# Gathering the first expert block inside the router, and stacking the halves of h in second blocks' down product

## The chip, the cores and the metric

One core of one Trainium2 chip runs the whole kernel, in one launch. The metric is the device time of that launch in microseconds; of several runs the median is given.

## The reference, cut to what matters

One inference step of a hybrid decoder layer over T = 1056 tokens (1024 of a prompt, 32 of samples). The change touches the last part, a mixture of 16 experts with top-2 routing, and the tables that lead to it:

```python
h = rmsnorm(x)
# top-1 group of 4, then top-2 of 4 experts in it; weights wts
# token-expert pairs sorted by expert into blocks of rows
out = (silu(xb @ w_eg[e]) * (xb @ w_eu[e])) @ w_ed[e]     # D=1024, FF=512
x = x + sum over the two pairs of a token (weight * out)
y = rmsnorm(x)                                            # final norm
```

All is fp32. Ahead of it stand an SSM and a gMLP mixer and a cross-attention, which the change leaves alone.

## The kernel before, in words

A product keeps fp32 accuracy on TensorE by splitting both factors into a high part (rounded to the fp32r format by a copy on ACT) and a low part (the rest, a subtraction on DVE), and summing three products: high x high, high x low and low x high (`product`, L4036 to L4038).

**The router's block** (`router_programs`, L3183) makes the normed rows h, stores them to DRAM (`h_scr`, SP, L3298) and computes the choice of experts. Its tail is a long chain of small operations on DVE: picks (L3605 to L3634), a prefix sum over tokens on PE (L3450, L3453), counts and block starts (L3645 to L3656), a slot for each token-expert pair (L3657 to L3663), its fields (L3665 to L3680), and one-hot matrices of block and lane (L3681 to L3687; POOL makes one third, L3357). Eighteen products on PE (L3462) turn these into tables: `m.tab` and `m.row`, the row that each lane of each block holds, and `m.tw`, its weight (DVE, L3689 to L3692). `keep_busy` (L129) issues idle products on PE. SP loads the six 1 MB pieces of expert 0's weights (four of gate and up, two of down) while that goes on (`load_piece`, L3756). Then all engines meet at a barrier.

**The experts' block** (`stage_experts`, L3763). Each expert has one block of 128 lanes and, if it has more rows, blocks of 64 lanes ahead of it (called second blocks here; `m.more` says how many). A block goes through these steps:

- POOL reads the block's column of `tab` and gathers its rows of `h_scr` into `e_x` (`gather`, L3922, L3925); PE turns them (`turn`, L4023); ACT and DVE split them into `e_xT` (`turned`, L4157, L4294).
- PE multiplies by gate and up (`hidden`, 48 products of 512 columns). A second block has only 64 lanes, so the high and low halves of x stand side by side as 128 lanes (`hidden_split`, L4063, L4064, 32 products) and DVE adds the two halves of the result (`gated_split`, L4311 to L4321).
- SiLU on ACT, the product with up on DVE; PE turns h (`turn_h`, L4104); ACT and DVE split it (`e_hT_high`, `e_hT_low`, L4325; for second blocks at the even lanes alone, L4330).
- PE multiplies by down (`down`, 24 products for a block of either kind). ACT scales the result by `m.tw` into `e_out` (`out`, L4202), POOL adds it by an indirect DMA to `res_scr` (`finish`, L3935) and waits until it has landed.

PE is one block ahead of itself: it takes the hidden product of block b+1, then the down product of block b, then turns h of b+1. The weights of the next expert are split meanwhile: a piece is loaded (SP), its high half made (ACT, L4157), its low half (DVE, L4298, for down pieces L4336), and the raw piece is then free, which lets SP load the same piece of the expert after. For expert e, `down_parts` waits on ACT for the down product of the expert before. The order on each queue is the order of the code: on ACT in a second block SiLU, x high, `out`, the down pieces, h high; on DVE in an expert's last block two low halves, the gating, x low, two low halves, h low.

At the start of the experts' block nothing of expert 0 is split yet, and its first rows are not gathered: POOL issues gathers 0 to 2 behind one another; PE runs 23 idle products (46 matmul instructions in the trace), turns block 0, runs 6 more, and starts. The second block's lanes are placed at even lane numbers, which the tables take into account:

```python
            g.keep_busy(UP, 23)
            turn(0)
            g.keep_busy(UP, 6)
            hidden(0, 0)
```

At the end the last two blocks are added without a trip through `res_scr`, and the final norm follows.

## Time and profile before

| | us |
|---|---|
| median of 3 runs | 1991.69 |
| lowest and highest | 1988.87 and 1991.7 |
| the profiled execution, its own time | 1985.8 |
| its span in the profile | 1983.7 |
| PE busy in the span | 1911.1 |
| DVE, ACT, POOL busy | 1015.7, 753.6, 410.3 |
| mean granted clock of TensorE | 0.989 of full |
| router's block ends, experts' block starts | about 1551.1 |
| first product of the experts | 1561.44 |

All times inside the profile are us from the start of the span. A matmul's own duration overlaps the next one's, so the distance from start to start is what a product costs. "Idle before" names the engine whose work ended the wait, and "issue" a wait for nothing that the profile shows.

### The profile page before, as it was taken

How to read it: one execution, taken by the hardware profiler on the slowest of the kernel's cores; microseconds unless marked ns; L12 is line 12 of the kernel's file. 1: busy time of each engine (PE TensorE's matmuls, PEld its weight loads, DVE VectorE, ACT ScalarE, POOL GpSimd, SP SyncE). 2: the span in 40 equal slices, each digit the busy share in tenths (PEclk: the TensorE clock that was granted, in tenths of full speed). 3: DMA queues.
4: the chain of work that ended last, by engine and by line, in shares of the span. 5: the costliest groups of instructions: out<-in, count | busy, mean ns of one | idle time of the engine just before them, and what ended most of it. 6: DMA issues, size and time to landing. Idle time of an engine off the chain costs nothing. (4 is left out here: it accounts for less than half of the span.)

```text
span 1983.7 us, 32313 instructions
## 1 busy us (share of the span) xinstructions
PE 1911.1 (96%) x11976; PEld 1717.4 (87%) x11977; DVE 1015.7 (51%) x1221; ACT 753.6 (38%) x1105; POOL 410.3 (21%) x513
## 2 busy tenths in 40 slices
PE   7999999999999999999999999999999799999995
PEld 5888999999999999889998899888788788887884
DVE  4314355554556565556114431445544666785786
ACT  4322132222244444633112232433321455774674
POOL 2000100000245455551011000000100222242225
PEclk9999999999999999999999999999999899999998
DMA  6121233334244434498434120446125387998997
GB/s 205 63 92 65 75 85 87 94 85 113 81 130 121 142 113 136 127 339 279 148 105 153 54 78 28 159 171 255 35 96 222 118 287 236 367 391 295 314 318 277
DMA packets 224593, 324.33 MB, mean 163 GB/s; under 512 B 15149, under 2 KB 158029, under 8 KB 224449
## 3 DMA queue, kind: packets, MB, share of 16 engines
q1 hardware_dynamic: 189924, 271.96, 40.2%
q0 software_dynamic: 7344, 25.38, 4.9%
q10 hardware_dynamic: 27232, 25.66, 3.7%
q8 instruction: 69, 1.13, 0.2%
q14 instruction: 24, 0.20, 0.0%
HBM read 250.97 MB, written 73.28 MB: 163 GB/s over the span
## 5 line engine op out<-in xcount | busy, mean ns | idle before, releaser
L4157 ACT ACTIVATE e_w_high<-big 128x2048 fp32r<-128x2048 f32 x94 | 175.5, 1910 | 37.7 <-PEq L3704 20.7
L286 PE MATMUL psum<-hT_high,t_w_high 128*128 128x352 f32 x528 | 171.2, 324 | 0.0
L288 PE MATMUL psum<-hT_high,t_w_low 128*128 128x352 f32 x528 | 170.1, 322 | 0.0
L287 PE MATMUL psum<-hT_low,t_w_high 128*128 128x352 f32 x528 | 170.1, 322 | 0.0
L4298 DVE TENSOR_TENSOR e_w_low<-big,e_w_high 128x2048 fp32r<-128x2048 f32 x64 | 143.8, 2288 | 34.8 <-ACT e_w_high L4157 27.4
L286 PE MATMUL psum<-hT_high,scan_w_high 128*128 128x352 f32 x384 | 131.3, 342 | 0.0
L288 PE MATMUL psum<-hT_high,scan_w_low 128*128 128x352 f32 x384 | 124.5, 324 | 0.0
L287 PE MATMUL psum<-hT_low,scan_w_high 128*128 128x352 f32 x384 | 123.8, 322 | 0.0
L4036 PE MATMUL psum<-e_w_high,e_xT 128*128 128x512 f32 x272 | 107.4, 395 | 3.1 <-DVE e_xT L4294 3.0
L4038 PE MATMUL psum<-e_w_high,e_xT 128*128 128x512 f32 x272 | 106.2, 390 | 0.0
L4037 PE MATMUL psum<-e_w_low,e_xT 128*128 128x512 f32 x272 | 106.0, 390 | 0.0
L286 PE MATMUL psum<-r_w_high,hT_high 128*128 128x512 f32 x256 | 101.8, 398 | 4.3 <-DVE hT_low L720 4.3
L287 PE MATMUL psum<-r_w_low,hT_high 128*128 128x512 f32 x256 | 100.7, 393 | 0.0
L288 PE MATMUL psum<-r_w_high,hT_low 128*128 128x512 f32 x256 | 100.7, 393 | 0.0
L286 PEld LDWEIGHTS psum<-hT_high,t_w_high 128*128 128x128 f32 x528 | 99.1, 188 | 0.1
L287 PEld LDWEIGHTS psum<-hT_low,t_w_high 128*128 128x128 f32 x528 | 99.1, 188 | 0.0
L288 PEld LDWEIGHTS psum<-hT_high,t_w_low 128*128 128x128 f32 x528 | 99.1, 188 | 0.0
L4336 DVE TENSOR_TENSOR e_w_low<-big,e_w_high 128x2048 fp32r<-128x2048 f32 x30 | 67.9, 2290 | 46.2 <-ACT e_w_high L4157 46.2
L1082 DVE SCALAR_TENSOR_TENSOR t_conv_out<-t_conv_in,veca,t_conv_out 128x1080 f32<-128x1080 f32 x60 | 80.6, 1344 | 7.5 <-DVE t_conv_out L1080 1.2
L1525 DVE TENSOR_SCALAR s_att<-psum 128x768 f32<-128x768 f32 x32 | 30.6, 958 | 100.0 <-PE psum L1333 100.0
L286 PE MATMUL psum<-yT_high,m_w_high 128*128 128x352 f32 x252 | 81.6, 324 | 0.0
L287 PE MATMUL psum<-yT_low,m_w_high 128*128 128x352 f32 x252 | 81.4, 323 | 0.0
(623 smaller groups left out, 4970.9 us busy)
## 6 DMA issues: line engine op xcount, KB each, us to landing
big<-in_w_expert_gate SPq DMA_DIRECT2D x32, 1024.0 KB, 7.1
big<-in_w_expert_up SPq DMA_DIRECT2D x32, 1024.0 KB, 10.1
big<-in_w_expert_down SPq DMA_DIRECT2D x32, 1024.0 KB, 12.0
t_w<-in_w_in SPq DMA_DIRECT2D x24, 512.0 KB, 4.7
m_gates<-gate_scr SPq DMA_DIRECT2D x22, 528.0 KB, 4.6
x_scr<-t_conv_out ACTq DMA_DIRECT2D x20, 512.0 KB, 4.8
gate_scr<-s_gate_tanh ACTq DMA_DIRECT2D x16, 528.0 KB, 3.3
scan_w<-in_w_gate SPq DMA_DIRECT2D x16, 512.0 KB, 4.1
```

Source lines behind the costliest of these rows:

```text
L286: nc.tensor.matmul(out, ah, w_h, start=start, stop=False)
L287: nc.tensor.matmul(out, ah, w_l, start=False, stop=False)
L288: return nc.tensor.matmul(out, al, w_h, start=False, stop=stop)
L1082: op = nc.vector.scalar_tensor_tensor(o, c[:, j:j + CB_OUT], wk[j], o, ALU.mult, ALU.add)
L1525: nc.vector.tensor_scalar(att[:, q].rearrange("p (b r) t -> p b (r t)", b=2), ps[:, RB:RB + 2, 0:XW], 0.0, None, ALU.min).then_inc(s_mn, 1)
L4036: nc.tensor.matmul(ps[:, bank, :], ah[:, k, :], w_h, start=(k == 0), stop=False)
L4037: nc.tensor.matmul(ps[:, bank, :], ah[:, k, :], w_l, start=False, stop=False)
L4038: mm = nc.tensor.matmul(ps[:, bank, :], al[:, k, :], w_h, start=False, stop=(k == kt - 1))
L4157: return nc.scalar.activation(dst, src, ACT.Copy)
L4298: nc.vector.tensor_tensor(wl[:, p, :], raw[:, p, :], wh[:, p, :].bitcast(F32), ALU.subtract).then_inc(s_wl, 1)
L4336: nc.vector.tensor_tensor(wl[:, p, :], raw[:, p, :], wh[:, p, :].bitcast(F32), ALU.subtract).then_inc(s_dl, 1)
```

## The change

First half. The 128 lanes of block 0 hold the first tokens of expert 0, in order, so they can be known from the prefix sums alone, without the tables. In the router's block, DVE makes a one-hot of each pick's place in expert 0, PE sums it into a row index with nine two-column products, POOL gathers the rows, PE turns them, and ACT and DVE split them. ACT also makes the high halves of expert 0's four gate and up pieces there, and DVE the first low half. The tiles for that get fixed addresses (`FirstBlock`). POOL also turns the table of steps so that it accounts for the moved lanes. The idle products at the start of the experts' block go.

Second half. For second blocks of experts 1 to 14, h is split into `e_hT_high`'s lanes 0 to 63 (high) and 64 to 127 (low), so that the down product is 16 products (`down_split`), and DVE adds the two halves (`out_summed`) before ACT scales 64 rows (`out_split`). Since the results now stand at lanes 0 to 63 and no longer at the even ones, four small products and a chain on DVE (`lanes_moved`) make a table for the scatter (`tab_o`) and move `m.tw`, at the start of the experts' block.

```diff
 router, POOL
+            pool.wait_ge(s_inl, 1)
+            nc.gpsimd.tensor_scalar(more0[:], nbk[:, 0:1], float(BASE), None, ALU.mult).then_inc(s_pv, 1)
...
+            nc.gpsimd.tensor_scalar(back[:], step[:], more0[:, 0:1], -float(BASE), ALU.is_le, ALU.mult).then_inc(s_pv, 1)
...
+            pool.wait_ge(ahead.s_index, 3)
+            for q in range(2):
+                pool.wait_ge(s_xst[q], 16 * ((NT + 1 - q) // 2))
+            nc.gpsimd.indirect_dma_start(
+                out=ahead.x[:], out_offset=None, in_=g.h_scr,
+                in_offset=bass.IndirectOffsetOnAxis(ap=idx0[:, 0:1], axis=0)).then_inc(ahead.s_x, 16)
 router, PE
+            pe.wait_ge(ahead.s_index, 1)
+            for c in range(NT):
+                mm = nc.tensor.matmul(ps[:, CN, 0:2], ahead.lanes[:, c, :], row0[:, c, :], start=(c == 0), stop=(c == NT - 1))
+            mm.then_inc(ahead.s_index, 1)
             g.keep_busy(3, 32)
+            pe.wait_ge(ahead.s_x, 16)
+            for k in range(DK):
+                at_k = (k % 2 * (DK // 2) + k // 2) * P
+                tr = nc.tensor.transpose(ps[:, TQ + k // 4, (k % 4) * P:(k % 4 + 1) * P], ahead.x[:, at_k:at_k + P], g.ident[:])
+            tr.then_inc(ahead.s_xt, 1)
             pe.wait_ge(s_ohl, 1)
 router, ACT
+            for p in range(ahead.HIGHS):
+                act.wait_ge(g.s_piece[p], 16)
+                nc.scalar.activation(ahead.wh[:, p, :], g.pieces[:, p, :], ACT.Copy).then_inc(ahead.s_wh, 1)
+            act.wait_ge(ahead.s_xt, 1)
+            nc.scalar.activation(ahead.xhl[:, :, 0, :], first_turned, ACT.Copy).then_inc(ahead.s_xh, 1)
 router, DVE, behind the prefix sums
+            ch.done(nc.vector.scalar_tensor_tensor(lane0, before0, 1.0, both[:, 0:NT, 0], ALU.add, ALU.mult))
+            nc.vector.scalar_tensor_tensor(ahead.lanes[:], mid(lane[:], NT), 1.0, last(lane0, P),
+                                           ALU.add, ALU.is_equal).then_inc(ahead.s_index, 1)
...
+            dve.wait_ge(ahead.s_index, 2)
+            ts(idx0[:], ps[:, CN, 0:1], float(T), None, ALU.add).then_inc(ahead.s_index, 1)
...
+            dve.wait_ge(ahead.s_wh, 1)
+            tt(ahead.wl[:, 0, :], g.pieces[:, 0, :], ahead.wh[:, 0, :].bitcast(F32), ALU.subtract).then_inc(ahead.s_wl, 1)
             dve.wait_ge(s_tb, 1)
...
+            dve.wait_ge(ahead.s_xh, 1)
+            tt(ahead.xhl[:, :, 1, :], first_turned, ahead.xhl[:, :, 0, :].bitcast(F32), ALU.subtract).then_inc(ahead.s_xl, 1)
 experts, POOL
-            for b in range(3):
+            pool.sem_inc(s_ix, 1)
+            for b in range(1, 2):
                 gather(b)
...
+            gather(2)
+            pool.wait_ge(s_lx, 9)
...
+            pool.wait_ge(s_far, MOVED)
 experts, PE
+            def down_split(b):
+                pe.wait_ge(s_hl, b + 1)
+                pe.wait_ge(s_oc, b)
+                for j in range(2):
+                    for k in range(FK):
+                        q, at = GU + k // (FK // 2), (k % (FK // 2)) * D + j * BANK
+                        nc.tensor.matmul(ps[:, DN + j, :], hth[:, k, :], wh[:, q, at:at + BANK], start=(k == 0), stop=False)
+                        mm = nc.tensor.matmul(ps[:, DN + j, :], hth[:, k, :], wl[:, q, at:at + BANK], start=False,
+                                              stop=(k == FK - 1))
...
-            g.keep_busy(UP, 23)
-            turn(0)
-            g.keep_busy(UP, 6)
+            lanes_moved()
             hidden(0, 0)
...
                 with pe.If(n > 0):
-                    with pe.Fori(0, n) as i:
+                    hidden_split(e, behind + 1)
+                    down(behind)
+                    turn_h(behind + 1)
+                with pe.If(n > 1):
+                    with pe.Fori(1, n) as i:
                         b = within(behind + i)
                         hidden_split(e, b + 1)
-                        down(b)
+                        down_split(b)
                         turn_h(b + 1)
                 b = within(behind + n)
                 hidden(e, b + 1)
-                down(b)
+                with pe.If(n > 0):
+                    down_split(b)
+                with pe.If(n < 1):
+                    down(b)
 experts, ACT: in an expert's last block, behind h_high(b)
+                    with act.If(n > 0):
+                        out_split(b)
+            def out_split(n):
+                act.wait_ge(s_ds, n + 1)
+                nc.scalar.activation(ob[0:XR], ob[0:XR], ACT.Copy, scale=m.tw[0:XR, bass.ds(n, 1)]).then_inc(s_oc, 1)
 experts, DVE: in an expert's last block, behind h_low(b)
+            def out_summed(b):
+                dve.wait_ge(s_dn, b)
+                dve.wait_ge(s_of, b)
+                nc.vector.tensor_copy(ob[0:XR], flat(ps[XR:P, DN:DN + 2, :])).then_inc(s_da, 1)
+                dve.wait_ge(s_da, b + 1)
+                nc.vector.tensor_tensor(ob[0:XR], ob[0:XR], flat(ps[0:XR, DN:DN + 2, :]), ALU.add).then_inc(s_ds, 1)
 experts, DVE, start
+            low(0, 1)
+            low(0, 2)
             nc.vector.tensor_scalar(far[:], m.row[:], float(SEQ), FAR, ALU.is_lt, ALU.mult).then_inc(s_far, 1)
...
-            low(0, 0)
-            low(0, 1)
-            turned(0)
-            low(0, 2)
             low(0, 3)
+            lanes_moved()
```

`lanes_moved` on PE is four products with 48 columns; on DVE it is ten small operations and two over 768 elements, the last two behind POOL's one-column copies (`s_lx`).

## Rows read from the trace of the kernel before

**Rows 1.** Page, part 1: busy time, share of the span and instructions of each engine.

```profile
PE 1911.1 (96%) x11976; PEld 1717.4 (87%) x11977; DVE 1015.7 (51%) x1221; ACT 753.6 (38%) x1105; POOL 410.3 (21%) x513
```

**Rows 2.** Windows: each engine's busy time (instructions), then granted clock, DMA share, GB/s.

```profile
1672.00:1684.00 12.00, 12.00 (x60) 10.03 (x58) 8.73 (x5) 9.14 (x7) 4.90 (x4) 1.00 0.54 125
1692.00:1804.00 112.00, 110.03 (x519) 91.00 (x518) 86.31 (x53) 75.38 (x54) 35.97 (x25) 1.00 1.03 377
```

**Rows 3.** Waits of PE from 1560 to the end: us in total, times, longest.

```profile
PE psum L4036 <- DVE e_xT L4294: 3.0, 2, 1.9
PE psum L4036 <- DVE e_hT_low L4330: 1.9, 1, 1.9
PE psum L4063 <- issue: 1.2, 1, 1.2
```

**Rows 4.** Chain of waits in order of time, at the seam: start, length, what.

```profile
1551.27 6.93 PE psum L129 x46
1558.20 0.89 PE psum L4023 x8
...
1560.16 1.24 DVE e_xT L4294
...
1561.44 0.50 PE psum L4036
```

**Rows 5.** Timeline, end of the router's block and start of the experts', by engine.

```profile
1545.89 4.08 PE L3462 MATMUL psum<-o_block_onehot,o_lane_onehot 128*128 128x144 f32 x18 [5.79 <-DVE o_block_onehot L3686]
...
1541.00 1.37 DVE L3682 TENSOR_TENSOR o_lane_onehot<-o_lane_of,o_lanes 128x1152 fp32r<-128x1152 f32 x1
...
1550.02 0.27 DVE L3689 TENSOR_SCALAR tab<-psum,o_spare_row 128x48 uint32<-128x48 f32 x1 [3.00 <-PE psum L3462]
...
1551.17 3.71 ACT L4157 ACTIVATE e_w_high<-big 128x2048 fp32r<-128x2048 f32 x2 [20.75 <-PEq L3704]
...
1552.55 1.27 POOL L3925 DMA_INDIRECT e_x<-h_scr,e_idx  x1 [0.95 <-POOL e_idx L3922]
```

**Rows 6.** Windows of low granted clock (the third value from the right is the clock's).

```profile
1544.30:1554.50 10.20, 7.32 (x33) 7.18 (x34) 5.46 (x11) 3.33 (x2) 1.48 (x2) 0.50 0.00 0
1810.50:1813.90 3.40, 3.40 (x10) 2.62 (x9) 3.40 (x3) 3.40 (x4) 3.02 (x2) 0.50 0.35 93
```

**Rows 7.** Groups by form from 1551 to 1940: busy, mean ns, idle before.

```profile
L4157 ACT ACTIVATE e_w_high<-big 128x2048 fp32r<-128x2048 f32 x94 | 175.5, 1910 | 37.7 <-PEq L3704 20.7 <-DMA big<-in_w_expert_down 12.3 <-DMA big<-in_w_expert_gate 3.5
L4298 DVE TENSOR_TENSOR e_w_low<-big,e_w_high 128x2048 fp32r<-128x2048 f32 x64 | 143.8, 2288 | 34.8 <-ACT e_w_high L4157 27.4 <-issue 7.4
...
L4311 DVE COPY e_silu<-psum 64x512 f32<-64x512 f32 x6 | 4.2, 693 | 8.4 <-PE psum L4064 5.6 <-issue 2.8
```

**Rows 8.** Timeline around the second of the six second blocks, PE, DVE; SP at the third.

```profile
1651.00 0.27 PE L4023 MATMUL psum<-ident,e_x 128*128 128x128 f32 x1
...
1657.37 0.60 PE L4104 MATMUL psum<-ident,e_h 128*128 128x128 f32 x4
1657.73 0.48 PE L4063 MATMUL psum<-e_w_high,e_xT 128*128 128x512 f32 x1
...
1659.37 0.69 DVE L4325 TENSOR_TENSOR e_hT_low<-psum,e_hT_high 128x512 fp32r<-128x512 f32 x1
...
1682.66 0.38 SPq L3756 DMA_DIRECT2D big<-in_w_expert_gate  x1
```

**Rows 9.** Timeline, POOL's gather with least room and the transposes that use its rows.

```profile
1863.42 1.00 POOL L3925 DMA_INDIRECT e_x<-h_scr,e_idx  x1 [0.80 <-POOL e_idx L3922]
...
1873.91 1.03 PE L4023 MATMUL psum<-ident,e_x 128*128 128x128 f32 x8
```

**Rows 10.** DMA from 1624 to 1936: every queue with packets, MB, share; a gather's landing.

```profile
q1 hardware_dynamic: 21138, 81.51, 67.3%
q0 software_dynamic: 5219, 19.02, 24.2%
...
e_x<-h_scr,e_idx POOLq DMA_INDIRECT x18, 7.4
```

171 lines of the change are left out of this document (133 added, 38 removed).

## The prediction, made blind

> **What bounds the kernel now.** I read the page first: PE is busy for 1911.1 us of the span [rows 1], so almost nothing can be won but by giving PE less to do or by closing its few gaps. Both halves of the change lie in the last fifth: the first is about the seam between the router's block and the experts' block, the second about PE's products inside the expert loop. Next I read the experts' stretch by the share of the DMA engines. Just before 1684 us they are half idle (0.54, 125 GB/s), then they are full for 112 us at a stretch (1.03, 377 GB/s) [rows 2]. In that stretch the weights set the pace and PE runs beside them. The waits of PE say where it shows: 3.0 us on the split x (two waits, both around the first blocks), 1.9 us in one wait on the split h behind late down weights, 1.2 us of issue at one branch, and nothing else of size until the end [rows 3]. The seam is seen best in the chain of waits: from the start of the experts' block to the first product it is 6.93 us of idle products that only keep PE busy, 0.89 of transposes, ACT's and DVE's split of x (from 1559.09 to 1561.40), in all 10.17 us from 1551.27 to 1561.44 [rows 4]. PE waits there for a gather that POOL could issue only at 1552.55 [rows 5].
>
> **The first half, step by step.** Taken off the path: the gather, its transposes, the split of x and the wait for them, 10.17 us. Put on it:
> - DVE, before the tables: one comparison over 128x1152 as in L3682, 1.4 us, and two small operations of about 0.2 (L3689 takes 0.27 with 48 columns) [rows 5]: 1.8 us, and all behind it on DVE moves by that, with POOL's products and PE's table product.
> - The low half of x at the end of DVE's router program, 1.24 us [rows 4], behind the tables, and so ahead of the barrier.
> - Four small products (the lanes' move) on PE ahead of the first real one, each at about 0.11 us by the eight transposes in 0.89 [rows 4], some 0.5.
>
> So PE would restart at 1551.27 + 1.8 + 1.24 = 1554.3 and reach its first product at 1554.9 in place of 1561.44: 6.5 us earlier.
>
> Costed at nothing: the four high halves of the weights on ACT (4 x 1.91 [rows 7]) lie in ACT's 20.75 us of idleness [rows 5]; the first low half on DVE (2.29 [rows 7]) lies in the 3.00 us in which DVE waits for the table product [rows 5]. The three low halves left for the new block need 2.3, 4.6 and, behind three small operations, 7.5 us, and PE asks for them 2.8, 5.5 and 8.3 us after its first product (12 products of 0.23 each time [rows 8]), itself 0.6 after the start. That cover is thin: each is ready about a microsecond early or less. The gather moves to about 1539; by its old landing (issued 1552.55, used from 1558.20 [rows 4, 5], 5.6 us) its rows are there by 1545, when PE is idle anyway ahead of the table product (5.79 us [rows 5]). The table of moved lanes on DVE is two operations over 768 elements (about 0.9 each by L3682) and some ten of 0.2, nearly 4 us, so DVE is done about 11.5 us into the block; PE's first two products take 11 us, and the gate times up needs DVE only after them. POOL waits for it before its loop; its first scatter is due later still. Its eight one-column copies move from behind the second gather to ahead of the third, and must only finish before DVE's last two of these operations. SP's first weight loads of the next expert depend on DVE's low halves and go out about 1 us earlier to 5 us earlier, into DMA engines that have room.
>
> What must be paid back is the clock. TensorE's granted clock is 0.50 from 1544.3 to 1554.5, that is 1.2 GHz, since PE had nothing to do ahead of the table product; it was back at 2.4 GHz after PE had run its idle products for 3.3 us [rows 4, 6]. Those paid for the rise before; now the first real products will. A second low stretch, after the 1.9 us wait, lasted 3.4 us [rows 6]. At half speed such a stretch costs 1.7 us. I take it once. The Trainium skill, "TensorE: Matmul & The Clock Gate", section on what the clock gate does, says that the array falls to half rate when it has been idle and comes back only after it has been kept busy; by that rule, too, dropping the warm-up is not free, and without it the first half would be worth the full 6.5. Bounds: 0 (clock stays up, because the transposes now break the idle time) to 3.4 us (two stretches). First half: 6.5 - 1.7 = **4.8 us**.
>
> **The second half.** A down product of a second block is 16 products of 512 columns in place of 24. From the start of the transposes of x (1651.00) to that of the transposes of h (1657.37) are 6.37 us; less 0.89 for the eight transposes [rows 4], the 24 products take 5.5 us [rows 8], 0.23 each; eight less save 1.84. Six second blocks ran (DVE's 64-row copies come six times [rows 7]), each the only one of its expert: 11.0 us off PE. What comes back:
> - The third of them lies just ahead of the 112 us in which the DMA engines are full [rows 2]. The next weights are issued at 1682.66, just ahead of the transposes that end the hidden product [rows 8], so their place is set before this down product is begun; PE 1.84 us earlier behind it only waits 1.84 longer, where the 1.9 us wait is now [rows 3]. Lost: 1.8.
> - The fourth stands right behind that wait, with DVE running late on low halves: I take off 0.6.
> - The output of a second block: before, ACT alone, in one pass over 128x1024; now DVE copies and adds 64x1024 from PSUM, then ACT scales. 64x512 take 0.69 [rows 7], so each of the two is between 0.69 and 1.39; near the upper end, 1.25, since it is a length of data that doubles: 2.5 us, and on ACT 1.1 (over half of the 1.91 that 2048 columns take [rows 7]). It lies beside PE's next hidden product, 7.3 us of work or more, and the next down product needs it only then. But DVE does it behind its last low half of h, which at the second of the six ends at 1660.06 [rows 8]: 1660.06 + 2.5 + 1.1 = 1663.7, against 1657.37 - 1.84 = 1655.5, + 0.4 + 7.4 + 0.9 = 1664.2 (transposes, 32 products, transposes), when PE wants the banks. Half a microsecond to spare, three times (where experts with two blocks follow each other). Queued behind it: on ACT the next SiLU, which must wait for DVE anyhow; on POOL the scatter, about 2 us later, and with it a gather. That gather had 10.5 us to its transposes at the tightest place [rows 9], and among the experts it lands in 7.4 [rows 10]; 10.5 - 1.8 - 1.7 = 7.0. I take off 0.5 for both.
> - Two more branches in each of the 14 rounds. Lower end: 0 (L4104 to L4063, with a loop's end and branches between, takes 0.36, no more than four transposes [rows 8]); upper end: 1.23 each, the issue wait [rows 3]. Near the lower, 0.1, in ten rounds: 1.0. The Trainium skill, "Advanced Engine Details and Errata", Control Flow Timing, gives 108 ns for a compare and branch; by it the two in each round come to 2 to 3 us in all.
>
> Second half: 11.0 - 1.8 - 0.6 - 0.5 - 1.0 = **7.1 us**. Both: 11.9. The profiled execution took 1985.8 us (span 1983.7, 2.1 around it) and would take 1973.9. It is itself 5.9 below the median of the three runs shown (1991.69), and nothing in the sum depends on that; against the median, **1979.8 us**, rounded to 1979.5.
>
> **The rivals.** (a) Nothing comes back: the clock is up, the DMA-bound stretch does not swallow the third product. 6.5 + 11.0 = 17.5, so 1974. Against it: the full DMA engines. Chance 0.17. (b) Transfers and outputs swallow more: later scatters make gathers late, or later experts too are paced by weights; only three of the six are kept, 5.5 - 1.5 in place of 7.1, together 8.8 off, 1983; worse with x late at three places, 1985. For it: 0.5 us margins. Chance 0.15. (c) The seam gives half: DVE's low halves or the lanes' table stop PE, or the clock stays low through two stretches: 6.5 - 3.4 - 1.5 = 1.6, total 8.7, 1983. Chance 0.12. (d) It doesn't do what it says: the first rows still land behind the tables and PE waits in the router's block; the seam is worth nothing and only 3 us of the rest survive: 1988.5. Chance 0.05. (e) Slower: PE stalls for its instructions. The loop body grows by half (one more copy of a hidden product and two more down products), and every round jumps over more of it. If each of the 14 rounds pays the 1.23 us that one jump paid [rows 3], that is 17.2 against 11.9: 1997; it decides from 0.85 us a round. Against it: from 1624 to 1936 the DMA queues show no instruction packets at all, only the two data queues [rows 10], so the whole loop is held. The Trainium skill, "Runtime: NRT & Kernel Launch", Instruction fetch mechanics, warns that a taken branch outside what is held must first fetch its target; on these rows nothing in the loop does so. Chance 0.05. The forecast keeps 0.46.
>
> **How the numbers follow.** A measurement of this kernel tells about 0.2% from no change, 4 us: faster means below 1987.7. The range runs from (a) taken from the lowest of the runs shown, 1988.87 - 17.5 = 1971.4, to the worse end of (b), 1985; left out are (d), (e) and tails of (b) and (c). Faster 0.87 = 0.46 + 0.17 + 0.15 + 0.12, less 0.03 for tails; same 0.07; slower 0.06.
>
> **What would show it.** Right: the first L4036 product some 6 us earlier and its first dozen spaced 0.43; transposes of the first rows in the idle gap ahead of the table product; 16 products, 3.7 us, in six down products; a longer wait for the split h behind the full DMA stretch, about 3.7 in place of 1.9. Wrong: waits of PE for e_out or e_xT after second blocks (b), instruction packets inside the loop (e), a first product that waits on a low half of weights (c), or no low clock there (a).

## The result, and the profile after

The changed kernel takes **1998.57 us** (median of 6 runs, 1995.99 to 2001.43); the kernel before took 1990.28 in the same rounds (1987.48 to 1992.35). The ratio is 1.0044, with a 95% interval of 1.0033 to 1.0056: **8.3 us slower**, where 11.9 faster was forecast, outside the range of 1971.4 to 1985.5. All comparisons with the kernel before are against its runs on the same chip. The profiled executions lie 12.7 us apart (1998.49 against 1985.8), because the one of the kernel before is 4.5 us below its median; so the rows below account for more than the 8.3 us.

The page of the changed kernel, part 1, part 3 (queue 8 brings instructions), and the head of part 4:

```profile
PE 1906.4 (96%) x11896; PEld 1710.7 (86%) x11897; DVE 1036.3 (52%) x1250; ACT 752.8 (38%) x1105; POOL 435.9 (22%) x519
...
q8 instruction: 69, 1.13, 0.2%
...
DMA 7%; PE 5%; issue 3%; DVE 2%; POOL 2%; ACT 1%; POOLq 0%; SPq 0%; DVEq 0%; ACTq 0%
DMA res_scr<-e_out,e_rows 6%; PE psum L4118 1%; PE psum L4120 1%; PE psum L4119 1%; DMA e_x<-h_scr,e_idx 1%; DVE e_w_low L4419 1%; DMA big<-res_scr 1%; POOL e_x L4003 1%; ACT e_w_high L4266 1%; POOL e_idx L4000 0%; POOL e_rows L4009 0%; PE 
```

PE has 4.7 us less to do than in [rows 1], and the span grew by 12.5 us, to 1996.2. The chain that ended last now leans on the landing of scatters: 6% of the span, 0% before. The waits of PE from 1550 us on show where PE stands still, against the 3.0, 1.9 and 1.2 of [rows 3]:

```profile
PE psum L4105 <- DMA e_x<-h_scr,e_idx: 5.6, 2, 3.5
PE psum L4118 <- issue: 5.3, 4, 2.1
PE psum L4180 <- PEq L3758: 3.2, 1, 3.2
PE psum L4208 <- DVE e_h L4428: 2.9, 3, 1.5
PE psum L4145 <- issue: 2.5, 3, 1.7
PE psum L4202 <- ACT e_out L4324: 2.4, 1, 2.4
PE psum L4118 <- DVE e_xT L4415: 1.9, 1, 1.9
```

**The seam did what was forecast.** The router's prefix product starts at 1532.28 us before and at 1536.25 after; nothing ahead of it is changed, and over the profiles of this study it starts anywhere from about 1531 to 1539, so stretches are counted from there. To the turn of block 1 it took 40.17 us before (1572.45) and takes 35.48 now (1571.73): 4.7 us gained, 4.8 forecast. The timeline of PE at the start of the experts' block:

```profile
1557.47 0.46 PE L4180 MATMUL psum<-row,ident 128*64 128x48 f32 x4 [3.16 <-PEq L3758]
...
1558.07 0.80 PE L4118 MATMUL psum<-e_w_high,e_xT 128*128 128x512 f32 x1
1558.66 0.63 PE L4119 MATMUL psum<-e_w_low,e_xT 128*128 128x512 f32 x1
1559.09 0.63 PE L4120 MATMUL psum<-e_w_high,e_xT 128*128 128x512 f32 x1
```

The first product stands 3.4 us earlier than in [rows 4] and 7.3 earlier counted from the prefix product, and from the second to the thirteenth they are 0.43 apart, at half clock.

**The loss is made among the experts and in the tail.** Counted by the transposes that turn each x, the changed kernel is 0.7 us ahead at block 1 and 1.8 ahead at 1651 us; it is 0.2 behind one second block later, 2.0 at 1718, 5.3 at 1806, 7.4 at 1892, and 12.5 at the end. (These are plain times in the span; counted from the prefix product it is 4.7 ahead at block 1 and 8.4 behind at the end.) This is the second of the six second blocks, in the timeline, the place at which the prediction worked its margins out [rows 8]:

```profile
1655.58 0.66 PE L4208 MATMUL psum<-ident,e_h 128*128 128x128 f32 x4 [1.50 <-DVE e_h L4428]
1657.93 0.50 PE L4145 MATMUL psum<-e_w_high,e_xT 128*128 128x512 f32 x1 [1.69 <-issue]
...
1654.85 0.68 DVE L4428 TENSOR_TENSOR e_h<-e_silu,psum 128x512 f32<-128x512 f32 x1
...
1660.98 0.68 DVE L4446 TENSOR_TENSOR e_hT_low<-psum,e_hT_high 128x512 fp32r<-128x512 f32 x1
1661.70 1.23 DVE L4458 COPY e_out<-psum 64x1024 f32<-64x1024 f32 x1
1662.96 1.21 DVE L4460 TENSOR_TENSOR e_out<-e_out,psum 64x1024 f32<-64x1024 f32 x1
...
1664.30 1.15 ACT L4317 ACTIVATE e_out<-e_out,tw 64x1024 f32<-64x1024 f32 x1 [7.42 <-DVE e_out L4460]
...
1666.26 1.60 POOL L4013 DMA_INDIRECT res_scr<-e_out,e_rows  x1 [7.35 <-ACT e_out L4317]
1675.41 0.18 POOL L4000 COPY e_idx<-tab 128x1 uint32 x1 [7.55 <-DMA res_scr<-e_out,e_rows]
...
1675.00 1.12 ACT L4311 ACTIVATE e_out<-psum,tw 128x1024 f32<-128x1024 f32 x1 [6.65 <-POOLq L4017]
1676.01 3.71 ACT L4266 ACTIVATE e_w_high<-big 128x2048 fp32r<-128x2048 f32 x2
...
1677.95 4.50 DVE L4497 TENSOR_TENSOR e_w_low<-big,e_w_high 128x2048 fp32r<-128x2048 f32 x2 [7.89 <-ACT e_w_high L4266]
```

Read it as a ring, that is, a circle of waits. The output is done by DVE behind its last low half of h, then by ACT; POOL scatters it 17.0 us after PE turned x at 1649.22 (in the kernel before 8.6 after). POOL waits until it has landed. There is one buffer `e_out`, so ACT's next output waits for that landing too (6.65 us), and **on ACT's queue the high halves of both down pieces, h and the SiLU stand behind it**; DVE's low halves wait for those, the gating stands behind the low halves, and PE waits for e_h at the next second block. Before, POOL had waited for PE at most blocks; now its index copy waits for a landing 17 times, 135.2 us in all (8 times, 76.5 before), and POOL seldom gets ahead again.

**The end of the kernel hangs on the last landing.** The final norm loads `res_scr` (SP) only when the last scatter has landed. From that load to the end it takes 38.4 to 40.6 us in every trace of this study. What differs is what the last scatter had waited for. Before, with PE's last turn of x:

```profile
1935.86 2.08 POOL L3935 DMA_INDIRECT res_scr<-e_out,e_rows  x1 [1.55 <-ACT e_out L4202]
1943.99 4.71 SPq L3908 DMA_DIRECT2D big<-res_scr  x9
1945.23 1.03 PE L4023 MATMUL psum<-ident,e_x 128*128 128x128 f32 x8
```

In the changed kernel:

```profile
1946.94 2.79 POOL L4013 DMA_INDIRECT res_scr<-e_out,e_rows  x1 [0.84 <-POOL e_rows L4009]
1952.07 1.03 PE L4105 MATMUL psum<-ident,e_x 128*128 128x128 f32 x8
1955.74 4.21 SPq L3986 DMA_DIRECT2D big<-res_scr  x9
```

Before, the chain of waits runs through PE's products up to 1933.8 and leaves for the scatter only then. In the changed kernel it leaves PE at 1900.3, at the last second block: ACT's and DVE's splits, DVE's sum, ACT's scaling, then three landings with POOL's own work between them:

```profile
1912.84 9.65 DMA res_scr<-e_out,e_rows
1928.99 10.62 DMA res_scr<-e_out,e_rows
1946.94 8.52 DMA res_scr<-e_out,e_rows
```

From PE's last turn of x to the end it is 38.5 us before and 44.1 after. So 5.6 of the 12.5 us are lost where PE waits for nothing: POOL is late, and the end with it.

### The profile page after: what moved, and what is told of

Its sections match the earlier page's. It is cut to its first block and busy times, and to the rows that moved or that the text cites. A ratio compares the mean times of both kernels' runs of the same rounds, so it can differ in the third digit from the quotient of the medians.

```text
span 1996.2 us, 32291 instructions
## 1 busy us (share of the span) xinstructions
PE 1906.4 (96%) x11896; PEld 1710.7 (86%) x11897; DVE 1036.3 (52%) x1250; ACT 752.8 (38%) x1105; POOL 435.9 (22%) x519
## 5 line engine op out<-in xcount | busy, mean ns | idle before, releaser
L4266 ACT ACTIVATE e_w_high<-big 128x2048 fp32r<-128x2048 f32 x90 | 167.9, 1910 | 8.4 <-DMA big<-in_w_expert_up 3.8
## 6 DMA issues: line engine op xcount, KB each, us to landing
big<-in_w_expert_down SPq DMA_DIRECT2D x32, 1024.0 KB, 11.9
```

Source lines behind the costliest of these rows:

```text
L4266: return nc.scalar.activation(dst, src, ACT.Copy)
```

## The experiments

A theory and three rivals were at hand, named by letters that the expectations use. **L**: the late output, through the one buffer and POOL's loop. **D**: DVE's 2.4 us more per second block. **B**: the branches and doubled bodies. **S**: the seam upsets the stretch after it.

### Each half alone, the output moved early, and the output made late in the kernel before

`first_only` takes the changed kernel and puts the second half back (old `h_high_split`, `out` for all, `down` for all, `tab`, no `lanes_moved`). `second_only` puts the second half on the kernel before.

> The first half of the change alone: block 0 gathered, turned and split inside the router's block; down products, outputs and the tables for rows as in the kernel before. Theory L (the first half gives what was forecast, and the loss sits in the late output of second blocks, which holds the one output buffer): 4 to 5 us faster than before, some 1985.5 us, with the stretch from the router's prefix product to the turn of block 1 at 35.5 us as in the changed kernel (40.2 before) and the experts' turn times after it at the spacing of before. Rival S (the seam itself upsets the stretch after it: the three weight pieces or the first gathers come late and the loss grows from there): no faster than before, 1990 us or more, the head start of 4.7 us gone by block 10. Rival B (branches and extra bodies cost, the halves do not matter): the branches are gone here, so about 1985.5 as well; the next run tells it apart.

> The second half alone, on the kernel before: high and low h of a second block stacked, its output summed by VectorE from two partition halves, the tables of moved lanes. Theory L: about 13 us slower than before (the 8.3 us of the whole change plus the 4.7 us which the seam gives), some 2003 us, with ScalarE waiting 5 to 8 us for the output buffer before the next main block's output, and GpSimd's index copy waiting for a scatter in well over 8 blocks. Rival S: about what before takes or faster (1983 to 1991), since the seam is undone.

```diff
 # sum_early, DVE, last_of
                     turned(b + 1)
+                    if split:
+                        with dve.If(n > 0):
+                            out_summed(b)
                     low(e + 1, 2)
                     low(e + 1, 3)
...
                 h_low(b)
-                if split:
-                    with dve.If(n > 0):
-                        out_summed(b)
 # late_out, on the kernel before, ACT, last_of of a split expert
+                    h_high(b)
+                    with act.If(n > 0):
+                        act.wait_ge(s_hl, b + 1)
+                        out(b)
```

> The changed kernel with one move: after a second block, VectorE adds the two halves of the output right behind its split of the next x, ahead of the last two low pieces of the next expert and of low h. Theory L: the sum is done at about 1625.3 instead of 1630.1 in the second second block, the scatter goes out 3 to 4 us earlier, near where before issues it, and most of the 12 to 13 us comes back: 1984 to 1990 us. Rival D (VectorE's extra 2.4 us per second block are the cost, wherever they stand, because the low pieces then come late for TensorE): within 2 us of the changed kernel, 1997 to 2001, with TensorE waiting for low pieces. Rival B (branches): the same 1997 to 2001, without such waits.

> The kernel before with one move: the output of a second block is copied by ScalarE only once VectorE has made the low half of the next h (as late as in the changed kernel, some 4 to 5 us later than before); nothing else differs, no stacked product, no branch on TensorE, no sum. Theory L: lateness alone makes most of the loss: 8 to 15 us slower than before, 1998 to 2005. Rivals D and B: within 2 us of before, since neither VectorE nor the branches have anything more to do.

| run | median | before | ratio, 95% interval |
|---|---|---|---|
| first_only | 1984.72 | 1988.97 | 0.9979, 0.997 to 0.9988 |
| second_only | 2012.24 | 1988.97 | 1.0115, 1.01 to 1.0131 |
| sum_early | 1990.48 | 1988.97 | 1.001, 0.9999 to 1.0021 |
| late_out | 1990.78 | 1988.97 | 1.0009, 1.0 to 1.0018 |

The first half alone is worth 4.2 us, so S falls and the second half costs the changed kernel some 12 to 14. On the kernel before it costs 23: one wait that the first half hides shows there, for the table of moved lanes, which stands ahead of the gating on DVE and which the prediction costed at nothing. The timeline of PE in `second_only`:

```profile
1582.52 1.11 PE L4135 MATMUL psum<-ident,e_h 128*128 128x128 f32 x4 [9.78 <-DVE e_h L4363]
```

The early sum brings 8 us back, as L said, but `late_out` cost 1.8 us, hardly clear of nothing, where L had said 8 to 15: **L as stated fell**. In its trace the scatter goes out 11.1 us after the turn of x and has landed at 21.7, with ACT waiting 4.93 us for it, and PE for nothing there. The kernel before itself has 8.6 and 21.1. So there is slack, and the changed kernel's 17.0 is beyond it.

### What TensorE's saving is worth, and two repairs

```diff
 # short_down: first_only, with the changed kernel's branches on PE and its down_split (16 products)
 # full_down: the changed kernel, with one more product in down_split
-                        mm = nc.tensor.matmul(ps[:, DN + j, :], hth[:, k, :], wl[:, q, at:at + BANK], start=False,
+                        nc.tensor.matmul(ps[:, DN + j, :], hth[:, k, :], wl[:, q, at:at + BANK], start=False, stop=False)
+                        mm = nc.tensor.matmul(ps[:, DN + j, :], hth[:, k, :], wh[:, q, at:at + BANK], start=False,
 # x_first: sum_early, DVE
                     low(e + 1, 0)
-                    low(e + 1, 1)
                 gated(b)
                 if not final:
                     turned(b + 1)
+                    low(e + 1, 1)
 # gather_ahead: sum_early, POOL
                     in_=ob[:], in_offset=None, compute_op=ALU.add).then_inc(s_o, 16)
+                with pool.If(before - b > 1):
+                    gather(b + 4)
                 pool.wait_ge(s_o, b * 16 + 16)
...
+            gather(3)
             with pool.Fori(0, before) as b:
-                gather(b + 3)
                 finish(b)
```

> The first half alone, as in the run of that name, and TensorE's down products of second blocks cut from 24 to 16 by leaving out the products of low h with high weights; outputs, splits, tables and VectorE's work stay as before (the result lacks that third of the product; what is left is the saving of the stacked product without its price). The forecast's arithmetic (11.0 us saved on TensorE, of which 1.8 lost to late weights): 8 to 9 us faster than the first half alone, some 1976 us. Theory X (what is next after the down product is VectorE's split of the next x, which stands behind two low pieces of the next expert, so TensorE gets to it earlier and waits): at most 3 us faster than the first half alone, 1981 to 1985, with four to six waits of 1.2 to 2.1 us ahead of the first hidden product after a second block.

> The changed kernel whole, but with 24 products instead of 16 in the down product of second blocks (high h with high weights twice, so the result is changed); all that the other engines do is as in the changed kernel. The forecast's arithmetic: 11 us slower than the changed kernel, some 2009 us. Theory X: the saving is swallowed by the waits for the split of x, so taking it away costs little: 1998 to 2003, and the waits ahead of the hidden products are gone.

> The run with the early sum, with one more move: VectorE gates h and splits the next x ahead of the second low piece of the next expert instead of behind it. Theory X: the waits of 1.3 to 2.0 us ahead of the hidden products (11.2 us in 7 in that run's trace) go, and 4 to 9 us come back: 1981 to 1986, at or below the first half alone. Rival D (VectorE has too much to do, whatever comes first): the same waits come back ahead of the second half of the gate products, and the time stays within 2 us of 1990.5.

> The run with the early sum, with GpSimd's loop turned: behind the scatter of a block it issues the gather of the x four blocks on, and only then waits for the scatter to land, so a landing no longer holds the gather. Theory P (the loss that is left after the early sum comes from GpSimd's chain of scatter, landing and gather, about as long as a block): 2 to 5 us faster than with the early sum alone, 1986 to 1988, no wait of TensorE for gathered x, index copies waiting for TensorE instead of for a scatter. Theory X: within 1 us of it, 1990 to 1991.5, since in that run's trace TensorE never waits for a gather.

| run | median | before | ratio, 95% interval |
|---|---|---|---|
| short_down | 1980.61 | 1989.33 | 0.9962, 0.9949 to 0.9976 |
| full_down | 1997.37 | 1989.33 | 1.0043, 1.0029 to 1.0056 |
| x_first | 1996.25 | 1989.33 | 1.0031, 1.0018 to 1.0043 |
| gather_ahead | 1997.28 | 1989.33 | 1.004, 1.0026 to 1.0053 |

`short_down` has everything that the second half gives and nothing that it adds outside PE (its result lacks low h times high weights): 4.1 us below the first half alone, where the forecast's arithmetic said 8 to 9. It has the changed kernel's branches on PE and is the fastest run of all, so those branches do not make the loss. And in the changed kernel 24 products (a wrong result again) take no longer than 16: nothing of the saving is left there. The runs of one kernel spread by 2 to 4 us (standard deviation), so with 5 to 12 of them a difference of two medians is known to 2 or 3 us. Part of why the saving shrinks shows in the `first_only` timeline, against the rows above:

```profile
1650.18 0.68 DVE L4384 TENSOR_TENSOR e_h<-e_silu,psum 128x512 f32<-128x512 f32 x1
...
1654.72 0.60 PE L4184 MATMUL psum<-ident,e_h 128*128 128x128 f32 x4
1655.08 0.48 PE L4143 MATMUL psum<-e_w_high,e_xT 128*128 128x512 f32 x1
```

Here e_h is ready (1650.86) 3.9 us before PE turns it, and the next product follows the transposes by 0.36. In the changed kernel e_h is ready at 1655.53, PE turns it 0.05 later, and the product comes 2.35 after that, with e_xT ready 1.26 before it. The same distances come back wherever PE has caught up with e_h, in the traces of `first_only`, `sum_early`, `one_late` and the changed kernel: 2.4 us from e_h to a second block's first product, 2.8 to a main block's. Between the two lie the end of the round, two register loads and the branches. So **the loop's own overhead is hidden as long as e_h is some 2.5 us early, and a shorter down product takes that cover away**. By the rows it is that path, and not the split of x as theory X had it, since e_xT was ready 1.26 to 1.68 us before each of those products. No run took the branches out, so this is read from the rows and not tested. Nor is it the whole of it. Between the turn of block 1 and the last turn of x, `short_down` is 3.1 us shorter than `first_only` in the traces, of 11.0 saved; the distances from the transposes of h to the next product have grown by 3.0 in all, one more stretch of low clock costs 1.7, and there are two waits that `first_only` has not, 1.5 for a gather and 1.2 for e_h.

Both repairs missed their forecasts, by 10 us. In `x_first` low pieces were late, and POOL's ring closed in the stretch where the DMA engines are full. Its timeline:

```profile
1750.01 2.90 POOL L4013 DMA_INDIRECT res_scr<-e_out,e_rows  x1 [0.84 <-POOL e_rows L4009]
1761.17 1.21 POOL L4000 COPY e_idx<-tab 128x1 uint32 x1 [8.27 <-DMA res_scr<-e_out,e_rows]
1763.18 3.05 POOL L4003 DMA_INDIRECT e_x<-h_scr,e_idx  x1 [0.80 <-POOL e_idx L4000]
1766.22 1.97 POOL L4009 COPY e_rows<-e_rows_to 128x1 uint32 x1
1769.03 2.90 POOL L4013 DMA_INDIRECT res_scr<-e_out,e_rows  x1 [0.84 <-POOL e_rows L4009]
```

That round is 19.02 us long and waits for nothing but its own landing; PE's round of a 128-lane block is 17.7. So in this trace a POOL that enters the stretch behind loses 1.3 us a block, and PE then waits for gathers (5.61 us at the longest, at 1879). In the changed kernel four such rounds take 73.1 us, 18.3 each. `gather_ahead` took the gather out of the ring (no wait of PE for gathered x is left) and put the release of `e_out` behind it: ACT waits up to 7.6 us for that. One hold was traded for the other.

### VectorE's load, the sum in another form, and the clock

```diff
 # idle_sums: first_only, DVE, where the changed kernel has its sum; nobody waits for it
+                nc.vector.tensor_tensor(r1[0:XR], rr[0:XR], rr[0:XR], ALU.add).then_inc(s_da, 1)
+                dve.wait_ge(s_da, b + 1)
+                nc.vector.tensor_tensor(r1[0:XR], rr[0:XR], rr[0:XR], ALU.add).then_inc(s_ds, 1)
 # one_sum: ACT, ahead of h_high
+                nc.scalar.activation(ob[0:XR], flat(ps[XR:P, DN:DN + 2, :]), ACT.Copy,
+                                     scale=m.tw[0:XR, bass.ds(n, 1)]).then_inc(s_da, 1)
 # one_sum: DVE, between low(e + 1, 2) and low(e + 1, 3)
+                nc.vector.scalar_tensor_tensor(ob[0:XR], flat(ps[0:XR, DN:DN + 2, :]), m.tw[0:XR, bass.ds(b, 1)], ob[0:XR],
+                                               ALU.mult, ALU.add).then_inc(s_oc, 1)
 # early_full: sum_early with 24 products; first_keep: first_only, PE, end of the router's block
             mm.then_inc(s_tb, 1)
+            g.keep_busy(3, 18)
```

> The first half alone, and VectorE in each second block's place does two additions of 64x1024 into a spare buffer behind its low half of h, where the changed kernel has its sum; nobody waits for them, the output goes out on time and the down product is whole. Rival D (VectorE's 2.4 us of extra work are the price): 4 to 8 us slower than the first half alone, 1989 to 1993. Theory L (the price is that the output is late, not that VectorE is busier): within 1.5 us of it, 1984 to 1986.

> The run with the early sum, with 24 products again in the down product of a second block (high h with high weights twice, so the result is changed). If the saving on TensorE is worth in this kernel what it is worth in the run of the short down product (4.1 us): 1994 to 1996. If nothing of it is left, as in the changed kernel (1997.4 with 24 products against 1998.6): 1989 to 1992.

> The changed kernel with the output of a second block made otherwise: ScalarE copies the weighted low half in the place where the kernel before has its output (ahead of high h), and VectorE adds the weighted high half to it in one operation, between the last two low pieces of the next expert; ScalarE has no more to do than before and VectorE 1.2 us per second block instead of 2.4. Theory L (what counts is when the scatter goes out): it goes out at most 1 us later than with the first half alone, and the time is 1981 to 1987, below the early sum by 4 us or more. Rival D: about half of VectorE's load stays, 1986 to 1990. Rival B (branches and the doubled bodies): 1990 as with the early sum.

> The first half alone, with 18 spare 128x128 products behind the table's products, at the end of the router's block, where TensorE then stands still for 3.4 us until the next block begins. In the trace of the first half the granted clock is 0.5 for the first dozen hidden products (0.43 us apart instead of 0.23), which makes 2.5 to 2.7 us. Theory C (the clock fell because TensorE stood still ahead of them): the spare products shorten the still time to about 1.3 us and the first products run 0.23 apart: 1981.5 to 1983. Rival (the switch of blocks or the wait for the split x sets the start of the stretch, and what is gained there is lost to the first weights' landing): within 1 us of 1984.7.

| run | median | before | ratio, 95% interval |
|---|---|---|---|
| idle_sums | 1984.5 | 1989.08 | 0.9973, 0.9961 to 0.9985 |
| early_full | 2001.25 | 1989.08 | 1.0059, 1.0044 to 1.0073 |
| one_sum | 1989.18 | 1989.08 | 0.9995, 0.9981 to 1.0009 |
| first_keep | 1982.34 | 1989.08 | 0.9957, 0.9944 to 0.9971 |

**D falls**: the extra load where nobody waits for it costs nothing (1984.5 against 1984.72). `early_full` came out above both of its forecasts and `one_sum` 2 us above the range of L. What TensorE's third product costs is no constant: 4.1 us without any late output, nothing in the changed kernel, 10.8 with the early sum (where DVE, waiting for the longer product, has low pieces behind it: PE waits 0.6 us for e_w_low twice; of the 12.0 between the two profiled executions, 6.1 come behind the last turn of x), and nothing again with one sum (`one_full`, below). The clock term stands: windows of `first_only`, then of `first_keep`, the third value from the right being the granted clock (0.50 is 1.2 GHz, 1.00 is 2.4 GHz):

```profile
1555.00:1559.00 4.00, 3.89 (x9) 3.17 (x10) 4.00 (x2) 1.28 (x1) 3.12 (x2) 0.50 0.79 265
```

```profile
1560.00:1564.00 4.00, 3.40 (x21) 2.88 (x21) 2.48 (x2) 0.82 (x1) 2.06 (x1) 1.00 0.33 94
```

PE stood still for 3.38 us ahead of the first, for 0.60 ahead of the second. So the clock did stay up. What that is worth is less sure. The medians say 2.4 us, but with 12 and 5 runs that is no more than their spread allows; in the traces the stretch from the prefix product to the turn of block 1 shrinks from 35.28 to 34.41, by 0.9, since the spare products also move the first product back by 1.2.

### Where the output stands

`one_sum` was no better than the early sum (1989.18), with runs from 1982 to 1995. Its place was moved both ways, at the same work:

```diff
 # one_late, ACT and DVE
+                    h_high(b)
                     with act.If(n > 0):
                         out_low(b)
-                    h_high(b)
...
                 h_low(b)
                 if split:
+                    with dve.If(n > 0):
+                        out_summed(b)
 # out_first: out_low ahead of high(e + 1, 3), out_summed ahead of low(e + 1, 2)
 # one_full: one_sum with 24 products; out_first_keep: out_first and g.keep_busy(3, 18)
```

> The run with one sum (ScalarE copies the weighted low half, VectorE adds the high half in one operation), with both put where the changed kernel has its output: ScalarE's behind high h, VectorE's behind low h. The work of every engine is that of the one sum; only its place differs. Theory L (the place alone makes the loss): 6 to 9 us slower than the one sum, 1995 to 1998, with ScalarE waiting for the output buffer. Rival W (the shorter chain of two operations instead of three is what helped, wherever it stands): within 2 us of 1989.

> The run with one sum, with the output put as far forward as it goes: ScalarE's half ahead of the fourth high piece of the next expert, VectorE's ahead of the third low piece. The scatter goes out 1 to 2 us earlier than with one sum, at or ahead of the time at which the first half alone sends it. Theory L, the last part of it: 1981 to 1985, at or below the first half alone (1984.7), since the stacked product then saves on TensorE and nothing is late. Rival V (VectorE now stands waiting for the down product with low pieces behind it): 1988 or more, with waits of TensorE for low pieces.

> The run with one sum, with 24 products again in the down product of a second block (result changed). If TensorE's saving counts once the output is not late: 7 to 11 us slower than one sum, 1996 to 2000 (with the early sum the third product more cost 10.8 us). If it is swallowed as in the changed kernel: within 2 us of 1989.

> The run with the output first and the 18 spare products at the end of the router's block. The two edits lie in different stretches and add up: 2.4 us below that run, 1979 to 1983, which would be below both kernels and at or below the first half with spare products (1982.3). Rival: what is gained at the seam is lost again in the stretch with the DMA engines full, so it stays within 1 us of the run without the spare products.

And last, one dose more and one addition:

```diff
 # later: one_late, DVE, in out_summed ahead of the sum; late_keep: one_late and g.keep_busy(3, 18)
+                nc.vector.tensor_copy(r1[0:XR], flat(ps[XR:P, DN:DN + 2, :]))
+                nc.vector.tensor_copy(rr[0:XR], flat(ps[XR:P, DN:DN + 2, :])).then_inc(s_ds, 1)
+                dve.wait_ge(s_ds, b + 1)
```

> The run with one sum put late, and two copies of 64x1024 into a spare buffer ahead of VectorE's sum: 2.4 us more between low h and the scatter. VectorE's extra work by itself cost nothing (idle sums). Theory G (what counts is when the scatter of a second block lands, counted from TensorE's transposes of the next x: 21.5 to 22.3 us in the run put late, 19.2 to 21.1 before, 23.5 to 26.3 in the changed kernel): the landings move to 24 us or more and most of the 15 us between the two kernels comes back, 1993 to 1999. Rival (a slack remains, or the three operations instead of two matter in another way): under 4 us more, 1984 to 1987.

> The run with one sum put late, with the 18 spare products at the end of the router's block. Both edits lie in different stretches: 1980.5 to 1982.5, some 2.4 us below the run put late and below the kernel before by 8 us. Rival (the gain at the seam is lost later): 1983 to 1985.

| run | median | before | ratio, 95% interval |
|---|---|---|---|
| one_late | 1983.51 | 1989.82 | 0.9969, 0.9959 to 0.9978 |
| out_first | 1993.32 | 1989.82 | 1.0015, 1.0002 to 1.0028 |
| one_full | 1988.39 | 1989.82 | 0.9991, 0.9983 to 1.0 |
| out_first_keep | 1990.93 | 1989.82 | 1.0012, 1.0 to 1.0023 |
| later | 1991.88 | 1989.63 | 1.0014, 1.0 to 1.0028 |
| late_keep | 1983.94 | 1989.63 | 0.9974, 0.9963 to 0.9985 |

`out_first` (forecast 1981 to 1985), `out_first_keep` (1979 to 1983) and `late_keep` (1980.5 to 1982.5) missed; `one_full` came within 2 us of `one_sum`, as in the changed kernel.

`one_late` was expected 6 to 9 us slower than `one_sum` and is 5.7 faster: the opposite of L. It is also the run in which **B falls**: it has the changed kernel's branches on all engines, its doubled bodies, its table of moved lanes and its stacked product, and differs from it only in the two operations that make the output, 15.1 us faster. When the scatter has landed orders the runs better than when it goes out, though not strictly, and the two are not the same. POOL's scatter of the second second block in `one_late`:

```profile
1658.18 1.60 POOL L4013 DMA_INDIRECT res_scr<-e_out,e_rows  x1 [4.75 <-DVE e_out L4459]
1668.19 0.18 POOL L4000 COPY e_idx<-tab 128x1 uint32 x1 [8.42 <-DMA res_scr<-e_out,e_rows]
```

and in `out_first`, with DVE's work beside it:

```profile
1658.17 4.48 DVE L4422 TENSOR_TENSOR e_w_low<-big,e_w_high 128x2048 fp32r<-128x2048 f32 x2
...
1659.05 5.07 POOL L4013 DMA_INDIRECT res_scr<-e_out,e_rows  x1 [2.91 <-DVE e_out L4460]
1673.55 0.18 POOL L4000 COPY e_idx<-tab 128x1 uint32 x1 [9.43 <-DMA res_scr<-e_out,e_rows]
```

Counted from the turn of x (1646.0 and 1650.9), the late one goes out 12.2 us after it and has landed at 22.2; the early one goes out at 8.2, needs 5.07 us on POOL in place of 1.60, and has landed at 22.7. It ends 1.47 us after DVE's pair of low halves; with the early sum (3.80 us long) and with one sum (2.87) it likewise ends 1.5 us after a low half, as if it had started there. Moving it forward buys no landing and puts two operations ahead of low pieces and h. The Trainium skill, "GPSIMD Engine Reference", Specifications, says that GpSimd's SBUF interfaces are shared with VectorE and contended by instructions with two SBUF inputs; the low halves are such instructions, and the trace agrees: 5.07 us beside them, 1.60 in `one_late`, where none runs during the scatter.

The table gives, all from timelines: from the turn of x at the second second block to the scatter and to POOL's next index copy after the landing; the time from PE's last turn of x to the end; and the profiled execution's own time beside the median.

| run | products | scatter out | landed | last turn to end | profiled | median |
|---|---|---|---|---|---|---|
| short_down | 16 | 7.5 | 19.5 | 38.7 | 1980.15 | 1980.61 |
| first_only | 24 | 8.6 | 19.6 | 38.6 | 1983.05 | 1984.72 |
| idle_sums | 24 | 8.6 | 20.4 | 38.6 | 1984.34 | 1984.5 |
| one_late | 16 | 12.2 | 22.2 | 39.4 | 1980.54 | 1983.51 |
| one_sum | 16 | 9.1 | 22.5 | 39.4 | 1990.21 | 1989.18 |
| one_full | 24 | 10.0 | 22.6 | 39.2 | 1990.33 | 1988.39 |
| sum_early | 16 | 9.8 | 22.7 | 39.7 | 1989.23 | 1990.48 |
| out_first | 16 | 8.2 | 22.7 | 45.8 | 1996.87 | 1993.32 |
| x_first | 16 | 10.6 | 24.5 | 45.2 | 1998.82 | 1996.25 |
| early_full | 24 | 11.1 | 24.8 | 45.8 | 2001.18 | 2001.25 |
| full_down | 24 | 15.5 | 25.2 | 45.3 | 2002.77 | 1997.37 |
| later | 16 | 16.6 | 25.7 | 44.3 | 1995.42 | 1991.88 |
| changed kernel | 16 | 17.0 | 26.2 | 44.1 | 1998.49 | 1998.57 |

`later` is the dose test: the landings move by 3 us or more and 8.4 of the 15 us between `one_late` and the changed kernel come back, less than the 10 or more that were expected. 4.9 us more stand behind the last turn of x. So the late landing is a cause, shown for about half of the way; what the changed kernel has beyond `later`, 6.7 us, is open.

The landing at one block does not explain the 5 to 10 us between `one_late` and the runs at 22.5 to 22.7. Two things in the traces do, as far as single executions tell. `out_first` against `one_sum`: from the turn of block 1 to the last turn of x both take 376 us; the last scatter then goes out 4.1 us ahead of the last turn instead of 9.3, and the end is 6.5 later. `one_late` against `one_sum`: the end behind the last turn is the same, and of the 6.4 us between the turns 5.1 are the clock's: `one_sum` has three stretches of about 3.4 us at half clock there, `one_late` none. A low clock does not follow every stall. The same wait of 1.94 us for e_xT ahead of block 1's products is followed by one in `first_only` and by none in the changed kernel; in `out_first` a wait of 2.58 us that ends at 1811.2 is followed by full clock:

```profile
1811.20:1816.20 5.00, 3.88 (x16) 2.89 (x16) 4.83 (x3) 4.97 (x4) 4.42 (x2) 1.00 0.19 45
```

So part of the order of these profiles is which of their stalls the clock fell on, and how much of the 5.7 us between the medians is that is open.

## Why the prediction was wrong

- **The seam** (6.5 - 1.7 = 4.8): right. Alone it measures 4.2; from the prefix product to the turn of block 1 it gains 4.7 us in the changed kernel's trace and 4.9 in `first_only`. That the clock would be low for the first dozen products came true. What it costs, 1.7 with bounds of 0 and 3.4, is not measured better than that: the spare products gave 2.4, 2.4 and -0.4 us in three pairs of medians, each with an uncertainty of 2 us or more.
- **The table of moved lanes, costed at nothing**: right as long as the first half stands. The cover was the early first product; without it there is one wait of 9.8 us (`second_only`). With the warm clock it is thin: in the trace of `late_keep` PE waits 2.06 us for e_h at 1570.95 and 0.78 for e_xT, where `one_late` waits 1.81 for e_xT in all, which takes back about 1 of the 1.9 us that the spare products had won.
- **Six times 1.84, 11.0 us, less 2.4 for late weights and less 1.0 for the branches**: the down products did shrink to 3.73 us (1619.09 to 1622.82), but `short_down` measures 4.1 where these terms leave 7.6. The term for the branches, 1.0, was too small: between the transposes of h and the next product `short_down` loses 3.0 us more than `first_only`. I had both ends, 0.1 and the 1.23 us of the one wait for issue in [rows 3]; neither holds for all rounds: it is nothing where e_h is early enough and 0.5 to 2.0 where it is not, since a shorter down product uncovers the end of the round. A second low stretch (1.7) and waits for a gather (1.5) and e_h (1.2) were not in the sum. The 1.8 for late weights did not show as forecast: the wait for the split h behind the full stretch is 1.7 us in `short_down`, not 3.7, and its lead of 3.3 us over `first_only` ahead of the stretch is still there at 1781.5, near the end of it.
- **"The output of a second block ... lies beside PE's next hidden product ... I take off 0.5 for both"**: the step that failed, and the one that turned the sign. Its durations were good (1.23 + 1.21 + 1.15 against 2.5 + 1.1). But it was held only against when PE wants the banks. The sentence on what is queued named "on ACT the next SiLU" and "on POOL the scatter, about 2 us later, and with it a gather". It did not follow the scatter to its landing, the landing to the one output buffer, and the buffer to ACT's next output with four pieces of work behind it. It did not follow the last landing to the final norm either, where 5.6 us were lost. Nor was the scatter 2 us later but 5.3 at the first second block (13.9 after the turn of x against 8.6) and 8.4 at the second (17.0), since a ring feeds its own lateness back. Against `short_down` the changed kernel is 18 us slower, where the forecast had 0.5 for it; the same output in two operations instead of three (`one_late`) is 2.9 slower.
- **The rivals.** (b) named the right place (late outputs, late gathers) at 1983 to 1985 and stopped before the sign turned; its sign of being wrong, waits of PE after second blocks, was not the one that showed most, since nearly half of the loss shows in no wait of PE. (e), the slower case, had a wrong mechanism: queue 8 brought 69 packets in both kernels, and no wait for instructions is seen. The slower rival should have been this ring: POOL's round, 12.2 us (the scatter at 1666.26 to the next) to 19.0, against PE's 14.2 and 17.7.

## What to carry to other kernels

When work moves behind a release, follow the release round to where it comes back: an output is not hidden because its reader is late, but only if the landing, the buffer and everything queued behind the next writer of that buffer are. Follow it to the end of the kernel too: a stage that starts on the last landing starts late even if the busiest engine never waited. A loop's own register loads and branches are free only while an engine is ahead of its data; an "issue" wait in the profile before is a first estimate of the price per round once it has caught up. Of the change keep the first half, with spare products ahead of the block switch (1982.34) or without (1984.72), or, with the stacked product, the output in two operations behind the splits (1983.51): all three beat both kernels, and their order among themselves is within the spread of the runs.

## What had not been expected of the hardware

- A scatter that POOL starts while DVE is already subtracting with two SBUF operands ends about 1.5 us after that subtraction, or after the next one if it follows at once: 2.87, 3.80 and 5.07 us long in three placements, against 1.60 where none runs at its start. Started 0.3 us ahead of a subtraction, as at 1610.62 in the kernel before, it keeps 1.60.
- A stall of 1.9 us can be paid twice. Windows of the run with the early sum, around a wait of 1.89 us that ends at 1760.00:

```profile
1757.00:1760.00 3.00, 1.11 (x7) 0.71 (x7) 3.00 (x3) 2.56 (x2) 0.66 (x2) 1.00 1.01 404
1760.00:1764.00 4.00, 4.00 (x11) 3.14 (x12) 4.00 (x3) 2.31 (x3) 2.84 (x1) 0.57 1.03 410
```

The granted clock is 0.57 for the four microseconds after it, and PE gets through 11 products there where 17 would fit at 0.227 us each: some 1.5 us more. The case above, 2.58 us and no fall, shows that the length of the stall alone does not decide it.
- One kernel's executions differ by up to 15 us (`later`, 1987 to 2002), more than most of the effects here. The profiled ones differ in how many stretches of low clock they have behind the turn of block 1: none in `one_late` and `idle_sums`, four in `sum_early`. One trace per kernel is not enough to rank kernels that lie this close.
